# Per-head state reads of the sample sequences: summed with the in-sequence part in token rows, turned once, behind the chunk states

## The chip, the cores and the metric

The kernel runs on one core of one Trainium2 chip. The metric is the device time in microseconds of one execution. A NeuronCore has TensorE (PE: matrix products, whose results go to PSUM), VectorE (DVE), ScalarE (ACT), GpSimd (POOL) and SyncE (SP, here the issuer of most DMAs). Every engine works through its own list of instructions in order; semaphores are what lets one wait for another.

## What is computed

One inference step of two layers, for a prompt of 512 tokens and for eight sample sequences of 8 tokens each. The change lies in layer 0, a gated linear recurrence with 8 heads (key width 128, value width 256):

```python
# S_t = diag(f_t) S_{t-1} + k_t v_t^T,   o_t = S_t^T q_t      (per head, S is 128 x 256)
b = jnp.cumsum(gc, axis=2)
A = jnp.einsum('bhtc,bhsc,bhtsc->bhts', qc, kc, jnp.exp(rel))       # causal, within a chunk
o = (jnp.einsum('bhts,bhsv->bhtv', A, vc)                          # in-sequence part
     + jnp.einsum('bhtc,bhcv->bhtv', qc * jnp.exp(b), S))          # read of the state
S_new = exp(b_last) * S + jnp.einsum('bhsc,bhsv->bhcv', kc * jnp.exp(b_last - b), vc)
...
o = rmsnorm(o, g_norm_w);  y = (o * jax.nn.silu(z)) @ w_out
```

For the sample tokens S is the state that came in, one for each sequence and head. Layer 1 is a dilated sliding-window attention, which the change leaves alone.

## The kernel before

All tokens (512 + 64) lie along the free axis and features on the partitions; layer 0 goes head by head. The code of each engine is written out by hand, so the order on each engine is the order of the text. Step h (`pe_step`, `act_step`, `dve_step`) holds the input projections of head h, the scan of head g = h-1 and the norm of head f = h-2. Steps 1 to 7 have all three kinds of work but for edges; step 8 has the scan of head 7 without new projections.

On PE, step h projects (lines 367 and 388, weights split into a high and a low part, `PJ` being four PSUM banks that take projections in turns), with the products of the scan between them. The scan uses the other four banks, `X`. First come eight levels of masked products q·k (line 1043, "grams"), which DVE merges into `at` (prompt) and `ats` (the 64 sample tokens, 64x64). Then comes `pe_states`:

- line 1055, the state reads: for each of the eight sequences n, the queries `qz` (32 columns, of which 8 are the tokens of n and 24 are zeros) against the state `s0`. A product of 32 columns uses a quarter of TensorE's columns, and four of them, for n mod 4 = 0 to 3, lie side by side. The result has token rows: sequence n at partitions 32·(n mod 4), columns 256·(n // 4) of bank 0.
- lines 1060 and 1061: five transposes that turn the keys `kh` to token rows (bank 3, and bank 1 for the samples).
- lines 1067 and 1069: for each half of the 256 value features, the in-sequence part `v_`·`ats`, in feature rows, and onto it the reads, which ACT has copied out as `orow` (line 816) and a product with picked columns of the identity turns into feature rows. This makes six products, in bank 2 from column 384.
- line 1076: four products of keys and values, the chunk states (banks 0 and 1).

ACT copies `orow` (128x512), then `kr` (the turned keys, line 818), then `os_` (the sample outputs in feature rows, line 822), and goes on with the exponentials of the next head's levels 5 to 7 (line 775). DVE makes `kz` from the turned sample keys (line 943), and after two more levels the scan of chunk states (lines 973 and 975) from `up_ready`, then low parts of weights (line 340). PE goes on with projections; the sample states follow in two parts (line 1083), the first behind `os_done`. Every product of float32 operands stands in the trace as two records of matmul and weight load, a transpose as one.

Of the kernel before, what the change touches and what calls it, by code (L numbers as in the profile page):

```python
# [10 lines left out]
ALU = mybir.AluOpType  # L11
ACT = mybir.ActivationFunctionType
AX_X = mybir.AxisListType.X

P = 128
# [3 lines left out]
DB, DS = 8, 8  # L19
TS = DB * DS  # L20
# [8 lines left out]
AH, ADK, ADV = 8, 128, 256  # L29
QKW, VW = AH * ADK, AH * ADV  # L30
CH = TP // P
# [94 lines left out]
def program(nc, I, O):  # L126
    with ExitStack() as ctx:
        def sb(name, shape, dt=F32, stack=ctx):
            return stack.enter_context(nc.sbuf_tensor(name, shape, dt))

        def sem(name):
            return ctx.enter_context(nc.semaphore(name))
# [13 lines left out]
        ident = sb("ident", [P, P])  # L146
# [9 lines left out]
        X = ctx.enter_context(nc.psum_tensor("X", [P, 4, 512], F32))  # L156
# [12 lines left out]
        ones_done, c_sig, c_silu, c_t, c_sb = (sem(x) for x in "ones_done c_sig c_silu c_t c_sb".split())  # L169
# [5 lines left out]
        q_sig, z_sig, k_done, g_done, b_done, eb_done, dl_done, qe_done = (  # L175
            sem(x) for x in "q_sig z_sig k_done g_done b_done eb_done dl_done qe_done".split())
# [4 lines left out]
        up_ready, up_read, os_ready, os_done = sem("up_ready"), sem("up_read"), sem("os_ready"), sem("os_done")  # L181
        ua_ready, ua_read, ub_ready, ub_read = sem("ua_ready"), sem("ua_read"), sem("ub_ready"), sem("ub_read")
        orow_ready, orow_done = sem("orow_ready"), sem("orow_done")
        op_ready, sq_done, ms_ready, ms_read, r_done, fin_done = (
            sem(x) for x in "op_ready sq_done ms_ready ms_read r_done fin_done".split())
        s0_in, s0_out, sp_out = [sem("s0_in0"), sem("s0_in1")], [sem("s0_out0"), sem("s0_out1")], sem("sp_out")
# [56 lines left out]
        def ticket_w(h, t):  # L243
            return TICKETS * h + t
# [98 lines left out]
        def wait_read(eng, t):  # L343

            eng.wait_ge(pj_read[t % 2], t // 2 + 1)
# [341 lines left out]
        st = ExitStack()  # L687
# [13 lines left out]
        v_ = sb("v_", [P, 2, CH + 1, ADV], stack=st)  # L701
        s0 = sb("s0", [P, 2, DB, ADV], stack=st)
# [4 lines left out]
        ats = sb("ats", [TS, TS], stack=st)  # L707
# [4 lines left out]
        os_ = sb("os_", [P, 2, TS], stack=st)  # L712
        v_low = sb("v_low", [TS, ADV], stack=st)
        qz = sb("qz", [P, 2, DB, 32], stack=st)
        orow = sb("orow", [P, 2 * ADV], stack=st)
        adr = sb("adr", [P, 512], stack=st)
        st.close()
        cond.close()
# [15 lines left out]
        def pool_scan(pool, h):  # L734
            b = h % 2
            pool.wait_ge(dl_done, h + 1)
            wait_read(pool, ticket_w(h, 0))
            seqs = lambda ap: ap[:, TP:T].rearrange("p (n t) -> p n t", t=DS)
            nc.gpsimd.tensor_tensor(qz[:, b, :, 0:DS], seqs(qe[:, b]), seqs(q_[:, b]), ALU.mult).then_inc(qe_done, 1)
            nc.gpsimd.tensor_tensor(qe[:, b, 0:TP], qe[:, b, 0:TP], q_[:, b, 0:TP], ALU.mult).then_inc(qe_done, 1)  # L740
# [16 lines left out]
        def act_step(act, chain, h):  # L757
            b, g, f = h % 2, h - 1, h - 2
# [53 lines left out]
                act.activation(v_[:, b, 0:CH, :].rearrange("p c v -> p (c v)"),  # L812
                               PJ[:, 0:2, :].rearrange("p e n -> p (e n)"), ACT.Copy).then_inc(pj_read[0], 1)
            if scan:
                act.wait_ge(orow_ready, g + 1)
                act.activation(orow[:], X[:, 0, :], ACT.Copy).then_inc(orow_done, 1)
                act.wait_ge(kt_ready, g + 1)
                act.activation(kr[:].rearrange("p c k -> p (c k)"), X[:, 3, :], ACT.Copy).then_inc(kr_done, 1)
                act.wait_ge(os_ready, g + 1)
                if g >= 1:  # L820
                    act.wait_ge(fin_done, 2 * g)
                act.activation(os_[:], X[:, 2, 384:512].rearrange("p (j t) -> p j t", j=2), ACT.Copy).then_inc(os_done, 1)
# [224 lines left out]
        def pe_states(pe, g):  # L1047

            b = g % 2
            pe.wait_ge(gram_read, 8 * g + 8)  # L1050
            pe.wait_ge(s0_in[b], 16 * (g // 2 + 1))
            pe.wait_ge(qe_done, 2 * g + 2)
            for n in range(DB):
                q = n % 4 * 32
                last = pe.matmul(X[q:q + 32, 0, n // 4 * ADV:(n // 4 + 1) * ADV], qz[:, b, n], s0[:, b, n],
                                 start=True, stop=True)
            last.then_inc(orow_ready, 1)
            pe.wait_ge(lv_done, XS * g + XS)
            for c in range(CH):
                pe.transpose(X[:, 3, c * P:(c + 1) * P], kh[:, c * P:(c + 1) * P], ident[:])  # L1060
            pe.transpose(X[0:TS, 1, 0:P], kh[:, TP:T], ident[:]).then_inc(kt_ready, 1)
            wait_read(pe, ticket_w(g, 3))
            wait_read(pe, ticket_w(g, 2))
            pe.wait_ge(orow_done, g + 1)
            for j in range(2):
                c0 = 384 + j * TS
                pe.matmul(X[:, 2, c0:c0 + TS], v_[0:TS, b, CH, j * P:(j + 1) * P], ats[:], start=True, stop=False)
                for x in range(2):
                    last = pe.matmul(X[:, 2, c0 + 32 * x:c0 + 32 * x + 32],
                                     orow[:, x * ADV + j * P:x * ADV + (j + 1) * P],  # L1070
                                     ident[:].rearrange("p (i t) -> p i t", t=32)[:, :, 0:DS], start=False, stop=(x == 1))
            last.then_inc(os_ready, 1)
            pe.wait_ge(kr_done, g + 1)
            pe.wait_ge(kz_done, g + 1)
            for c in range(CH):
                last = pe.matmul(X[:, c // 2, c % 2 * ADV:(c % 2 + 1) * ADV], kr[:, c], v_[:, b, c], start=True, stop=True)  # L1076
            last.then_inc(up_ready, 1)

        def pe_new_states(pe, g, b0, bank, ready):
            for i in range(2):  # L1080
                for x in range(2):
                    r = slice(32 * x, 32 * x + 32)
                    last = pe.matmul(X[:, bank + x, i * ADV:(i + 1) * ADV], kz[r, b0 + i], v_[r, g % 2, CH],  # L1083
                                     start=True, stop=True)
            last.then_inc(ready, 1)
# [14 lines left out]
        def pe_step(pe, h):  # L1100
# [42 lines left out]
            if scan:  # L1143
                pe_states(pe, g)
# [451 lines left out]
        def own(buf, b):  # L1596

            c0 = 32 * b - DS * (b % 4)
            return buf.rearrange("p b t -> p (b t)")[:, c0:c0 + 32]
# [624 lines left out]
        def load_attention_constants(sp):  # L2224
            for dst, src in ((cs_raw[:, 0], I["c_cos"]), (cs_raw[:, 1], I["c_sin"]), (swaps, I["c_swap"]),
                             *((there, src) for _, there, src in masks),
                             (qkw[:, 0], I["b_q_norm_w"].partition_broadcast(P)),
                             (qkw[:, 1], I["b_k_norm_w"].partition_broadcast(P))):
                sp.dma_start(dst, src).then_inc(a_const, 16)
# [103 lines left out]
        @block.gpsimd  # L2333
        def _(pool):
            nc.gpsimd.memset(ones[:], 1.0).then_inc(ones_done, 1)
            nc.gpsimd.memset(eps[:], EPS).then_inc(ones_done, 1)
            nc.gpsimd.memset(scT[:], 0.0).then_inc(ones_done, 1)
            for n in range(3):
                s = n % 2 * 2
                pool.wait_ge(n_sq, 2 * n + 2)  # L2340
                nc.gpsimd.tensor_tensor(nsq[:, s], nsq[:, s], nsq[:, s + 1], ALU.add).then_inc(sq_sum, 1)
            pool.wait_ge(n_ms, 5)
            nc.gpsimd.memset(qz[:], 0.0).then_inc(ones_done, 1)
            pool.wait_ge(ones_done, 4)
            pool.wait_ge(parked, 16)
            for h in range(AH + 1):
                if h < AH:
                    pool_scan(pool, h)
                if 1 <= h <= AH - 2:
                    pool.wait_ge(sq_done, h)  # L2350
                    nc.gpsimd.tensor_tensor(sq0[:, 0], sq0[:, 0], sq0[:, 1], ALU.add).then_inc(sum_done, 1)
            pool.wait_ge(n_lo, 2 * KD + 1)
            pool.wait_ge(n_hx, 2 * KD + 1)
            pool.wait_ge(parked1, 16)
            nc.gpsimd.memset(qs, 0.0).then_inc(zeros_done, 1)
            nc.gpsimd.memset(pz[:], 0.0).then_inc(zeros_done, 1)
            pool.wait_ge(zeros_done, 1)
            pool.wait_ge(tab_done, 1)
            for j in range(GH):
                for g in range(3):  # L2360
                    for c in range(3):
                        rope_pool(pool, j, g, c)
                for g in range(3):
                    pool.wait_ge(qkt_read, 3 * j + g + 1)
                    if j or g:
                        pool.wait_ge(st_ready, 4 * j + (0, 1, 3)[g])
                    nc.gpsimd.tensor_copy(qs[:, :, 0:DS], qkT[:, g, 0, TP:T].rearrange("p (b t) -> p b t", b=DB)).then_inc(qs_done, 1)
# [130 lines left out]
```

## Time and profile before

| | us |
|---|---|
| median of three runs | 1216.82 (1215.17 to 1216.98) |
| the profiled execution, its own time | 1211.92 |
| its span, first to last instruction | 1210.1 |
| PE busy | 1166.0 (96%) |
| DVE / ACT / POOL busy | 644.1 (53%) / 508.9 (42%) / 147.2 (12%) |
| mean granted TensorE clock, share of full | 0.991 |

The profiled execution took 4.9 us less than the median of the timed ones. A busy engine is not one at its peak: TensorE's records overlap, so its pace is read from the distance between the starts of two groups.

### The profile page before, as it was taken

How to read it: one execution, taken by the hardware profiler on the slowest of the kernel's cores; microseconds unless marked ns; L12 is line 12 of the kernel's file. 1: busy time of each engine (PE TensorE's matmuls, PEld its weight loads, DVE VectorE, ACT ScalarE, POOL GpSimd, SP SyncE). 2: the span in 40 equal slices, each digit the busy share in tenths (PEclk: the TensorE clock that was granted, in tenths of full speed). 3: DMA queues.
4: the chain of work that ended last, by engine and by line, in shares of the span. 5: the costliest groups of instructions: out<-in, count | busy, mean ns of one | idle time of the engine just before them, and what ended most of it. 6: DMA issues, size and time to landing. Idle time of an engine off the chain costs nothing.

```text
span 1210.1 us, 23191 instructions
## 1 busy us (share of the span) xinstructions
PE 1166.0 (96%) x9624; PEld 1093.9 (90%) x9624; DVE 644.1 (53%) x1222; ACT 508.9 (42%) x1026; POOL 147.2 (12%) x155
## 2 busy tenths in 40 slices
PE   6889999999999999989999899999999999999998
PEld 4689998999998999988999799999999999998998
DVE  2775657575848474757333563364346335526432
ACT  3552344434443434353211364464356435537221
POOL 1000000000000000000000063045016204500000
PEclk9899999999999999999999899999999999999999
DMA  9862534343443434421622336423643282362432
GB/s 259 283 201 70 157 92 140 110 132 104 120 126 106 143 105 127 122 92 40 218 70 71 131 111 156 129 74 90 143 125 84 77 193 83 84 133 72 150 106 59
DMA packets 243067, 147.90 MB, mean 122 GB/s; under 512 B 19337, under 2 KB 237449, under 8 KB 242450
## 3 DMA queue, kind: packets, MB, share of 16 engines
q1 hardware_dynamic: 228626, 134.62, 39.6%
q10 hardware_dynamic: 14336, 11.80, 3.0%
q8 instruction: 76, 1.25, 0.4%
q14 instruction: 29, 0.24, 0.1%
HBM read 124.37 MB, written 22.02 MB: 121 GB/s over the span
## 4 chain that ended last, share of the span: by engine, by line
PE 89%; DVE 4%; DMA 3%; SPq 2%; ACT 2%; issue 1%; DVEq 0%; ACTq 0%
PE PJ L367 24%; PE PJ L1473 17%; PE PJ L1188 14%; PE PJ L388 8%; PE X L1043 5%; DMA raw<-in_a_w_in_dram 2%; PE PJ L414 1%; PE X L1166 1%; PE X L1589 1%; PE X L1083 1%; PE X L1076 1%; PE PJ L1498 1%; PE X L1554 1%; PE X L1616 1%; PE X L1168 1%; PE X L1097 1%
## 5 line engine op out<-in xcount | busy, mean ns | idle before, releaser
L340 DVE TENSOR_TENSOR w_lo<-raw,w_hi 128x1024 fp32r<-128x1024 f32 (+1 forms) x128 | 156.7, 1238 | 176.1 <-ACT w_hi L332 175.4
L332 ACT ACTIVATE w_hi<-raw 128x1024 fp32r<-128x1024 f32 (+1 forms) x128 | 129.1, 1025 | 157.5 <-PE PJ L1473 73.0
L1473 PE MATMUL PJ<-w_hi,h_hi 128*128 128x256 f32 x600 | 167.5, 287 | 0.8 <-DVE w_lo L340 0.7
L1473 PE MATMUL PJ<-w_lo,h_hi 128*128 128x256 f32 x600 | 164.5, 283 | 0.0
L367 PE MATMUL PJ<-h_hi,w_hi 128*128 128x288 f32 (+1 forms) x736 | 161.5, 301 | 0.9 <-ACT v_ L812 0.9
L367 PE MATMUL PJ<-h_hi,w_lo 128*128 128x288 f32 (+1 forms) x736 | 157.6, 296 | 0.0
L367 PE MATMUL PJ<-h_lo,w_hi 128*128 128x288 f32 (+1 forms) x736 | 157.3, 295 | 0.0
L1473 PE MATMUL PJ<-w_hi,h_lo 128*128 128x256 f32 x480 | 135.7, 283 | 0.0
L367 PEld LDWEIGHTS PJ<-h_hi,w_hi 128*128 128x128 f32 x736 | 118.0, 189 | 5.5 <-issue 4.5
L367 PEld LDWEIGHTS PJ<-h_hi,w_lo 128*128 128x128 f32 x736 | 118.9, 189 | 0.0
L367 PEld LDWEIGHTS PJ<-h_lo,w_hi 128*128 128x128 f32 x736 | 118.8, 189 | 0.0
L1473 PEld LDWEIGHTS PJ<-w_hi,h_hi 128*128 128x128 f32 x600 | 114.9, 192 | 2.1 <-DVE w_lo L340 0.9
L1473 PEld LDWEIGHTS PJ<-w_lo,h_hi 128*128 128x128 f32 x600 | 115.0, 192 | 0.0
L388 PE MATMUL PJ<-w_hi,h_hi 128*128 128x256 f32 x320 | 93.0, 298 | 4.2 <-DVE w_lo L340 4.2
L1188 PE MATMUL PJ<-oz_low,w_hi 128*128 128x256 f32 x448 | 96.1, 296 | 0.0
L1473 PEld LDWEIGHTS PJ<-w_hi,h_lo 128*128 128x128 f32 x480 | 92.0, 192 | 0.0
L388 PE MATMUL PJ<-w_lo,h_hi 128*128 128x256 f32 x320 | 88.5, 284 | 0.0
L1188 PEld LDWEIGHTS PJ<-oz_low,w_hi 128*128 128x128 f32 x448 | 75.6, 190 | 0.0
L388 PE MATMUL PJ<-w_hi,h_lo 128*128 128x256 f32 x256 | 72.9, 285 | 0.0
L1017 DVE SCALAR_TENSOR_TENSOR xT<-PJ,ada,xT 128x128 f32<-128x128 f32 (+1 forms) x40 | 17.7, 497 | 103.4 <-PE PJ L1188 96.7
L775 ACT ACTIVATE dd<-dd 128x576 f32<-128x576 f32 (+1 forms) x64 | 41.3, 657 | 72.3 <-DVE dd L878 63.2
L388 PEld LDWEIGHTS PJ<-w_hi,h_hi 128*128 128x128 f32 x320 | 61.9, 193 | 8.0 <-DVE w_lo L340 4.4
(309 smaller groups left out, 2286.5 us busy)
## 6 DMA issues: line engine op xcount, KB each, us to landing
raw<-in_a_w_in_dram SPq DMA_DIRECT2D x48, 512.0 KB, 4.3
raw<-in_ada_w_dram SPq DMA_DIRECT2D x32, 512.0 KB, 3.8
raw<-in_b_w_in_dram SPq DMA_DIRECT2D x64, 256.0 KB, 3.3
kvc<-in_cache_kv_w_dram SPq DMA_DIRECT2D x24, 512.0 KB, 5.3
pre<-in_ada_w_dram SPq DMA_DIRECT2D x16, 512.0 KB, 8.3
s<-in_state_hgrn_dram SPq DMA_DIRECT2D x8, 1024.0 KB, 7.0
out_hgrn_sample_dram<-s ACTq DMA_DIRECT2D x8, 1024.0 KB, 5.2
raw<-in_a_w_out_dram SPq DMA_DIRECT2D x16, 512.0 KB, 4.6
```

Of the source, the lines that this page charges most:

```text
L332: act.activation(w_hi[:, i % SPLITS, 0:size], raw[:, n % RAWS, 0:size], ACT.Copy).then_inc(hi_done, 1)
L340: dve.tensor_tensor(w_lo[:, i % SPLITS, 0:size], raw[:, n % RAWS, 0:size], w_hi[:, i % SPLITS, 0:size].bitcast(F32), ALU.subtract).then_in ...
L367: last = nc.tensor.matmul(PJ[:, 2 * s + e, 0:n1 - n0], a[:, k, :], b[:, k, n0:n1], start=(k == 0 and i == 0), stop=(k == KD - 1 and i == 2))
L388: last = nc.tensor.matmul(out_of(tile), a, b[:, k % 4, :], start=(k == 0 and i == 0), stop=(k == KD - 1 and i == len(passes) - 1))
L414: last = nc.tensor.matmul(PJ[q:q + 32, bank, n % 4 * P:n % 4 * P + P], scT[:, k, :], w[:, k, :], start=(k < 4), stop=(k >= 4))
L775: act.activation(dd[:, x % 2, 0:n], dd[:, x % 2, 0:n], ACT.Exp).then_inc(exp_done, 1)
L1017: dve.scalar_tensor_tensor(out=x, in0=y, scalar=gate, in1=x, op0=ALU.mult, op1=ALU.add)
L1043: last = pe.matmul(X[:, i % 2, c * P:(c + 1) * P], left[:, c * P:(c + 1) * P], right[:, c * P:(c + 1) * P], start=True, stop=True)
L1076: last = pe.matmul(X[:, c // 2, c % 2 * ADV:(c % 2 + 1) * ADV], kr[:, c], v_[:, b, c], start=True, stop=True)
L1083: last = pe.matmul(X[:, bank + x, i * ADV:(i + 1) * ADV], kz[r, b0 + i], v_[r, g % 2, CH], start=True, stop=True)
L1188: last = pe.matmul(PJ[:, 2 * (t % 2) + e, 0:z - x], a[:, n % nk, :], b[:, x:z], start=(n == 0 and i == 0), stop=(n == 2 * nk - 1 and i == 2))
L1473: last = pe.matmul(PJ[:, tile // 2, tile % 2 * 256:tile % 2 * 256 + 256], a, b[:, k, :], start=(first and k == 0 and i == 0), stop=(kk == ...
```

## The change

The reads no longer go to two column ranges of bank 0 but are added up, for the sequences of one quarter, in bank 2, columns 0 to 255. This needs each sequence's 8 query columns at another place of its 32; `own(qz, n)`, which layer 1 already used, takes a window that starts 8·(n mod 4) columns early and so brings them there. The rows of the 64 sample tokens are then 0 to 63, and the sequences are dealt over the four quarters so that two lie in each: quarters 0 and 1 hold four of the sequences, quarters 2 and 3 the other four in rows 64 to 127. The in-sequence part is now one product, `ats` by `v_`, in token rows 0 to 63 (line 1059 of the changed kernel), and the reads of quarters 0 and 1 are added onto it.

`orow` is now 128x256. A new constant `twice` (128x64, made once by POOL as the sum of the identity's two halves of columns) turns it: one product for each half of the value features both turns it and adds rows 64 to 127 onto rows 0 to 63. These two products stand behind the chunk states, the transposes ahead of the reads. ACT copies `kr` first, then `orow`.

```diff
         if scan:
-            act.wait_ge(orow_ready, g + 1)
-            act.activation(orow[:], X[:, 0, :], ACT.Copy).then_inc(orow_done, 1)
             act.wait_ge(kt_ready, g + 1)
             act.activation(kr[:].rearrange("p c k -> p (c k)"), X[:, 3, :], ACT.Copy).then_inc(kr_done, 1)
+            act.wait_ge(orow_ready, g + 1)
+            act.activation(orow[:], X[:, 2, 0:ADV], ACT.Copy).then_inc(orow_done, 1)
             act.wait_ge(os_ready, g + 1)
...
         pe.wait_ge(gram_read, 8 * g + 8)
-        pe.wait_ge(s0_in[b], 16 * (g // 2 + 1))
-        pe.wait_ge(qe_done, 2 * g + 2)
-        for n in range(DB):
-            q = n % 4 * 32
-            last = pe.matmul(X[q:q + 32, 0, n // 4 * ADV:(n // 4 + 1) * ADV], qz[:, b, n], s0[:, b, n],
-                             start=True, stop=True)
-        last.then_inc(orow_ready, 1)
         pe.wait_ge(lv_done, XS * g + XS)
...
         wait_read(pe, ticket_w(g, 3))
+        pe.wait_ge(s0_in[b], 16 * (g // 2 + 1))
+        pe.wait_ge(qe_done, 2 * g + 2)
+        pe.matmul(X[0:TS, 2, 0:ADV], ats[:], v_[0:TS, b, CH, :], start=True, stop=False)
+        for i in range(2):
+            for q in (2, 3, 0, 1):
+                n = q % 2 * 4 + q // 2 * 2 + i
+                last = pe.matmul(X[32 * q:32 * q + 32, 2, 0:ADV], own(qz[:, b], n), s0[:, b, n],
+                                 start=(i == 0 and q >= 2), stop=(i == 1))
+        last.then_inc(orow_ready, 1)
         wait_read(pe, ticket_w(g, 2))
-        pe.wait_ge(orow_done, g + 1)
-        for j in range(2):
-            c0 = 384 + j * TS
-            pe.matmul(X[:, 2, c0:c0 + TS], v_[0:TS, b, CH, j * P:(j + 1) * P], ats[:], start=True, stop=False)
-            for x in range(2):
-                last = pe.matmul(X[:, 2, c0 + 32 * x:c0 + 32 * x + 32],
-                                 orow[:, x * ADV + j * P:x * ADV + (j + 1) * P],
-                                 ident[:].rearrange("p (i t) -> p i t", t=32)[:, :, 0:DS], start=False, stop=(x == 1))
-        last.then_inc(os_ready, 1)
         pe.wait_ge(kr_done, g + 1)
         pe.wait_ge(kz_done, g + 1)
...
+        pe.wait_ge(orow_done, g + 1)
+        if g == 0:
+            pe.wait_ge(ones_done, 5)
+        for j in range(2):
+            last = pe.matmul(X[:, 2, 384 + j * TS:384 + (j + 1) * TS], orow[:, j * P:(j + 1) * P], twice[:],
+                             start=True, stop=True)
+        last.then_inc(os_ready, 1)
```

PE's list around `pe_states` of head 0, before. The names are the tiles written and read:

```order
L438 MATMUL PJ<-fold,adr 128x9 x3
L1055 MATMUL X<-s,qz 32x256 [waits qe_done,s0_in0,gram_read]
L1055 MATMUL X<-s,qz 32x256 x7
L1060 MATMUL X<-ident,kh 128x128 [waits lv_done]
L1060 MATMUL X<-ident,kh 128x128 x3
L1061 MATMUL X<-ident,kh 64x128
L1067 MATMUL X<-ats,v_ 128x64 [waits orow_done,pj_read0,pj_read1]
L1069 MATMUL X<-ident,orow 128x32 x2
L1067 MATMUL X<-ats,v_ 128x64
L1069 MATMUL X<-ident,orow 128x32 x2
L1076 MATMUL X<-v_,kr 128x256 [waits kz_done,kr_done]
L1076 MATMUL X<-v_,kr 128x256 x3
```

The same place in the changed kernel:

```order
L438 MATMUL PJ<-fold,adr 128x9 x3
L1054 MATMUL X<-ident,kh 128x128 [waits lv_done,gram_read]
L1054 MATMUL X<-ident,kh 128x128 x3
L1055 MATMUL X<-ident,kh 64x128
L1059 MATMUL X<-v_,ats 64x256 [waits qe_done,s0_in0,pj_read1]
L1063 MATMUL X<-s,qz 32x256 x8
L1070 MATMUL X<-v_,kr 128x256 [waits kz_done,kr_done,pj_read0]
L1070 MATMUL X<-v_,kr 128x256 x3
L1076 MATMUL X<-twice,orow 128x64 [waits ones_done,orow_done]
L1076 MATMUL X<-twice,orow 128x64
```

The transposes moved ahead of the reads, and the turning products, two instead of six, behind the chunk states. On ACT, before:

```order
L816 ACTIVATE orow<-X 128x512 [waits orow_ready]
L818 ACTIVATE kr<-X 128x512 [waits kt_ready]
L822 ACTIVATE os_<-X 128x128 [waits os_ready]
L775 ACTIVATE dd<-dd 128x512 [waits sub_done] x2
L775 ACTIVATE dd<-dd 128x576 [waits sub_done]
```

and in the changed kernel:

```order
L817 ACTIVATE kr<-X 128x512 [waits kt_ready]
L819 ACTIVATE orow<-X 128x256 [waits orow_ready]
L823 ACTIVATE os_<-X 128x128 [waits os_ready]
L776 ACTIVATE dd<-dd 128x512 [waits sub_done] x2
L776 ACTIVATE dd<-dd 128x576 [waits sub_done]
```

The two first copies changed places and one of them is half as wide; `os_` and the three exponentials behind it stand where they stood.

## Rows read from the trace of the kernel before

**Rows 1.** The page's first part: busy time and share of each engine.

```profile
PE 1166.0 (96%) x9624; PEld 1093.9 (90%) x9624; DVE 644.1 (53%) x1222; ACT 508.9 (42%) x1026; POOL 147.2 (12%) x155
```

**Rows 2.** Busy time in one head's period, from one L1055 to the next.

```profile
core 0: us, PE busy (x) PEld busy (x) DVE busy (x) ACT busy (x) POOL busy (x), PEclk, DMA share, GB/s
130.52:193.88 63.36, 63.12 (x538) 58.66 (x538) 40.14 (x78) 26.32 (x35) 3.34 (x3) 1.00 0.40 119
```

**Rows 3.** Timeline of PE, head 1: start us, length us, line, tiles, form, records.

```profile
192.89 1.06 PE L438 MATMUL PJ<-fold,adr 128*128 128x9 f32 x8
193.88 1.07 PE L1055 MATMUL X<-s,qz 128*32 128x256 f32 x16
194.88 0.66 PE L1060 MATMUL X<-ident,kh 128*128 128x128 f32 x4
195.37 0.27 PE L1061 MATMUL X<-ident,kh 128*64 128x128 f32 x1
195.76 0.40 PE L1067 MATMUL X<-ats,v_ 64*128 64x64 f32 x2
196.09 0.63 PE L1069 MATMUL X<-ident,orow 128*128 128x32 f32 x4
196.66 0.43 PE L1067 MATMUL X<-ats,v_ 64*128 64x64 f32 x2
197.02 0.63 PE L1069 MATMUL X<-ident,orow 128*128 128x32 f32 x4
197.48 1.97 PE L1076 MATMUL X<-v_,kr 128*128 128x256 f32 x8
199.11 0.47 PE L388 MATMUL PJ<-w_hi,h_hi 128*128 128x256 f32 x1
199.41 0.28 PE L388 MATMUL PJ<-w_lo,h_hi 128*128 128x256 f32 x1
199.53 0.28 PE L388 MATMUL PJ<-w_hi,h_hi 128*128 128x256 f32 x1
```

**Rows 4.** Timeline of PE in layer 1, columns as in rows 3.

```profile
854.67 0.43 PE L1694 MATMUL X<-vr,oz 64*64 64x128 f32 x2
855.03 1.08 PE L1700 MATMUL X<-kvc,pz 128*32 128x128 f32 x32
856.04 1.09 PE L1589 MATMUL X<-ident,kvc 128*128 128x128 f32 x8
856.97 1.00 PE L1708 MATMUL X<-ident,oz 128*128 128x64 f32 x8
857.79 0.50 PE L367 MATMUL PJ<-h_hi,w_hi 128*128 128x256 f32 x2
```

**Rows 5.** Timeline of ACT in the same head; in brackets, idle us before and releaser.

```profile
195.02 0.60 ACT L816 ACTIVATE orow<-X 128x512 f32<-128x512 f32 x1 [1.57 <-PE X L1055]
195.68 0.60 ACT L818 ACTIVATE kr<-X 128x512 f32<-128x512 f32 x1
197.69 0.28 ACT L822 ACTIVATE os_<-X 128x128 f32<-128x128 f32 x1 [1.41 <-PE X L1069]
...
208.56 0.65 ACT L769 ACTIVATE oz<-PJ 128x576 f32<-128x576 f32 x1 [2.76 <-PE PJ L367]
```

**Rows 6.** Timeline of DVE in the same head.

```profile
195.68 0.68 DVE L943 TENSOR_TENSOR kz<-X,seqm 64x512 f32<-64x512 f32 x1 [1.50 <-PE X L1061]
...
203.61 2.35 DVE L340 TENSOR_TENSOR w_lo<-raw,w_hi 128x1024 fp32r<-128x1024 f32 x2
209.24 0.76 DVE L898 TENSOR_TENSOR oz<-PJ,oz 128x576 f32<-128x576 f32 x1 [3.29 <-ACT oz L769]
```

**Rows 7.** What SP's DMA queue waited for, 100 to 560 us: total, times, longest.

```profile
SPq L2292 <- PE PJ L414: 180.0, 28, 9.4
```

**Rows 8.** Timeline of ACT, then PE, in the last head.

```profile
557.68 0.28 ACT L822 ACTIVATE os_<-X 128x128 f32<-128x128 f32 x1 [1.41 <-PE X L1069]
...
559.38 1.13 PE L1083 MATMUL X<-v_,kz 32*128 32x256 f32 x8
```

More of the change, by code:

```diff
@@ L714, in program @@
         qz = sb("qz", [P, 2, DB, 32], stack=st)
-        orow = sb("orow", [P, 2 * ADV], stack=st)
+        orow = sb("orow", [P, ADV], stack=st)
+        twice = sb("twice", [P, TS], stack=st)
         adr = sb("adr", [P, 512], stack=st)
@@ L2345, in _ @@
             pool.wait_ge(parked, 16)
+            nc.gpsimd.tensor_tensor(twice[:], ident[:, 0:TS], ident[:, TS:P], ALU.add).then_inc(ones_done, 1)
             for h in range(AH + 1):
```

## The prediction, made before the changed kernel was run

> **What bounds the kernel now.** I read the shares first: PE is busy 96% of the span, DVE 53%, ACT 42% [rows 1]. A share is an average, so the next view is the busy time of one head's period. From one state read (L1055) to the next there are 63.36 us, the same to 0.01 us in six periods, of which one is shown, and PE is busy for 63.12 of them at the full granted clock; ACT works 26 us, DVE 40 us, the DMA engines are busy 0.40 of the time [rows 2]. So in layer 0 PE waits for nobody once it is under way, and what leaves its list leaves the time, unless something else becomes late. The third view is the timeline of PE through `pe_states` of one head [rows 3]; the same groups stand in all eight heads. The fourth is a place in layer 1 with the very kinds of products that the change brings [rows 4].
>
> The lengths in a timeline overlap, so I price by distances between starts. From the first read (193.88) to the second projection product behind the chunk states (199.41) there are 5.53 us. I take the second because the first L388 record is shown as starting before the chunk states are through: 0.30 us lie between the two where the next follows at 0.12.
>
> **What a change of shape costs.** The four records of L1069 stand twice in rows 3: from 196.09 to 196.66 (0.57 us) with a product of another form behind them (64 rows of the array instead of 128), and from 197.02 to 197.48 (0.46) with one of the same form. Leaving a form costs 0.11 us. Entering one costs something too, since its first weights can't be loaded under the work ahead: the four L1060 records take 0.49, at 0.11 each 0.44, so 0.05. L438 (8 records, 0.99) and L1708 (8 records, 0.82) differ by 0.17, about half at each end [rows 3, 4].
> The Trainium skill has a rule on this: the page TensorEngine Tiling, Key Properties, says that switching the tiling mode, other than going to another tile of the same mode, drains TensorE. The two L1069 groups agree with it for 128 to 64 rows. By that rule alone, counting forms in the two orders, seven switches become four, which speaks for the change, with about a third of the sum below; L1061 (64 columns behind 128) counts as a switch by it and shows none of the cost, in both kernels.
>
> **The changed stretch, term by term, per head.**
> - Entry. The transposes follow L438 in the same form, where the reads changed it. That saves 0.08 ahead of 193.88 (half of the 0.17), and the first load is hidden: the four transposes take 0.44.
> - The fifth transpose and the change to 64x64: 0.11 + 0.11, less a little as only 64 weight columns are loaded; 0.20. Before, 0.39 passed here (195.37 to 195.76), since PE waited for `orow`, whose copy ends at 195.62 [rows 5]. That wait is gone.
> - `ats` by `v_` in token rows, two records of 256 columns. No such row exists. L1694 is the same form with 128 columns and also has the 32-column reads behind it: 0.36 for two [rows 4]. 16 records of 256 columns (L1055) take 1.00 and 32 of 128 columns (L1700) take 1.01, both four abreast, so a step of 256 columns costs as much as two of 128, which is 0.11 more per record: 0.58. Bounds: 0.36, were it hidden beside the reads of the other two quarters, and 0.80.
> - The eight reads, 16 records: 1.00, as now with another form behind. That they add up in one bank makes no difference in L1700, which adds four such products in each quarter and runs at the pace named.
> - The chunk states. Now 197.48 to 199.41 less one step of 0.12: 1.81. They will follow a change of form, so 0.02 to 0.10 more; their first step is already a long one, I take 1.83. Their waits: the turned keys are ready about 0.8 us after the first transpose (194.88 to 195.68, where DVE starts on them) [rows 3, 6], and `kr` and `kz` take 0.60 and 0.68. Counted from the first transpose that is 1.4 and 1.5, while PE gets to the chunk states at 0.44+0.20+0.58+1.00 = 2.22. Covered, with 0.7 to spare; if `ats` and the reads took only 0.9 together, PE would begin to wait here.
> - The turning: two products of 64 columns, four records, at the pace of L1708 (0.82 for 8, nearly all of it one load each): 0.45. Its wait: `orow` can be copied once the reads have ended, with half the columns some 0.4 us (between the 0.28 of `os_` and the 0.60 of 512 columns), which lies beside the 1.83 of the chunk states. Covered.
> - The projection behind: from its first to its second product 0.20, an estimate between the 0.12 of its pace and the 0.30 of now [rows 3].
>
> The sum is 0.44+0.20+0.58+1.00+1.83+0.45+0.20 = 4.70, against 5.53, with 0.08 at the entry: **0.91 us less per head**. With the bounds of the terms it is 0.6 to 1.15.
>
> **Heads 0 to 6** sit inside steps with projections: 7 x 0.91 = 6.4 us.
>
> **The last head** has no projection behind; PE goes straight to L1083, which waits for `os_done`. Before, `os_` was copied by 557.96 under the chunk states [rows 8]. Now the turning is the last thing ahead of the wait, and behind its last record come its end (0.28), the copy (0.28) and two hand-overs, 0.7 us, where 0.33 were spent from the last chunk state. DVE also has oz_low to make ahead of `kz` there, which may keep PE 0.1 us. I put the gain at 0.2, bounds -0.2 and 0.5.
>
> **What the move makes late.** `os_ready` comes behind the chunk states. Before, ACT started `os_` at 197.69 [rows 5]; by the terms above the turning ends near 198.5, so ACT starts it 0.85 later, and three exponentials that are queued behind it, DVE's levels on these, its scan of the chunk states and its two low halves of weights (L340, 203.61 to 205.96) move by up to as much. DVE waits behind them 3.29 us for PE's projection by way of ACT, and ACT waits 2.76 itself [rows 5, 6]. PE now comes 0.91 earlier, so that these two waits shrink by about 1.8 and stay positive. The projection that needs the first low half starts behind that same wait, so it finds it there with over 1 us to spare. I cost the delay at nothing; the cover is 1.0 to 1.5 us. `kz` and `kr` are earlier by about 1.0, which helps DVE. The loads: SP's queue waits for PE to free buffers (180.0 us in 28 waits) [rows 7], so weights are not what is late. The new POOL instruction is 64 columns, once, where POOL has nothing else; it stands ahead of the `qz` of head 0, for which PE waits before anyway.
>
> **Sum.** 6.4 + 0.2 = 6.6 us. The profiled execution would go from 1211.92 to 1205.3 (its span from 1210.1 to 1203.5). The median shown is 4.9 us above the profiled one, nothing in the profile says why, and I take the same difference from it: 1216.82 - 6.6 = 1210.2, 0.54% less.
>
> **Rivals.**
> - Slower: the reads lose their four-abreast running, because the two rounds now write the same columns of a bank and two quarters add onto what `ats` left. Then 16 records go one after another at the pace of L1076 (1.81 for 8, 0.22 each): 3.6 instead of 1.00, 2.6 more, and 0.91 becomes a loss of 1.7 per head; times 8, 13.5 us: 1230. It turns the sign from the point where `ats` and reads take over 2.5 us together. L1700 does exactly this adding without such a loss [rows 4], with one difference: there each 64x64 product stands in the same chain as well. 4 in 100.
> - No change: ACT's late `os_`. If the 0.85 reached PE in each of the seven heads (through the exponentials, DVE and the low half of weights), 7 x 0.06 + 0.2 = 0.6 would be left: 1216.2. It needs the cover of 1.0 to 1.5 us worked out above to be false, for instance because ACT's other pieces don't move up with PE. 7 in 100.
> - Half the gain: something small waits in each head (chunk states for `kr` or `kz`, the turning for `orow`, or each change of form costs 0.1 more around the new order). 0.3 to 0.6 per head, 2.4 to 4.8 us: near 1213. 12 in 100.
> - The forecast: 0.6 to 1.15 per head, 4.5 to 8.5 us, 1208.3 to 1212.3: 77 in 100.
>
> **How the numbers follow.** The three timed runs before lie within 1.8 us, so the median of after can be off by about 1 us whatever the kernel; that widens the low end to 1207.6. The high end takes in part of the half-gain case: 1213.4. What a measurement can tell from no change is 0.2%, 2.4 us. Faster by over that: the forecast and most of the half-gain case, 0.86. Within: the late `os_` and the rest of it, 0.10. Slower: 0.04.
>
> **What would show it.** In the profile of the changed kernel: a head's period of 62.4 to 62.5 us instead of 63.36, with PE busy all but 0.2 of it; the reads at 1.0 us and not 3.6; about 0.58 from the `ats` product to the reads; the turning at 0.45; ACT's wait at its L769 row down from 2.76 to about 1, DVE's at the gate down by 1.8, and no new wait of PE. The forecast is wrong if PE shows idle time ahead of a projection, with DVE's low halves as the releaser, or if the step from one form to the next is longer than 0.2 us anywhere in the stretch.

## The result, and the profile after

The changed kernel takes 1207.16 us (median of 8 runs, 1204.88 to 1211.51) against 1214.88 us for the kernel before (8 runs on the same chips, 1212.12 to 1216.98): a ratio of 0.9938, 95% interval 0.9923 to 0.9952. It is faster by about 0.6%; the two medians lie 7.7 us apart. The prediction said faster, by 0.54% and 6.6 us, but gave the time as 1210.2 with a range of 1207.6 to 1213.4, and 1207.16 lies below that. What it said of the mechanism held in the main; its range for the time did not.

One head's period (busy time between two first transposes; start and end, length, then busy time and records of each engine, granted clock, DMA share) in the changed kernel:

```profile
core 0: us, PE busy (x) PEld busy (x) DVE busy (x) ACT busy (x) POOL busy (x), PEclk, DMA share, GB/s
130.98:193.37 62.39, 62.26 (x533) 57.66 (x533) 40.13 (x78) 26.11 (x35) 3.34 (x3) 1.00 0.39 116
```

This answers to [rows 2]: 62.39 for 63.36, the same in all six full periods, and PE still busy for all but 0.13 us. The saving is 0.97 us per head.

PE's timeline through the changed stretch of head 1, which answers to [rows 3]:

```profile
192.46 1.06 PE L438 MATMUL PJ<-fold,adr 128*128 128x9 f32 x8
193.37 0.63 PE L1054 MATMUL X<-ident,kh 128*128 128x128 f32 x4
193.84 0.27 PE L1055 MATMUL X<-ident,kh 128*64 128x128 f32 x1
194.04 0.64 PE L1059 MATMUL X<-v_,ats 64*64 64x256 f32 x2
194.62 1.07 PE L1063 MATMUL X<-s,qz 128*32 128x256 f32 x16
195.62 1.99 PE L1070 MATMUL X<-v_,kr 128*128 128x256 f32 x8
197.45 0.56 PE L1076 MATMUL X<-twice,orow 128*128 128x64 f32 x4
197.81 0.37 PE L388 MATMUL PJ<-w_hi,h_hi 128*128 128x256 f32 x1
198.02 0.28 PE L388 MATMUL PJ<-w_lo,h_hi 128*128 128x256 f32 x1
```

From start to start, against the terms of the sum:

| term | predicted | before | after |
|---|---|---|---|
| L438 to the next group | 0.08 less | 0.99 | 0.91 |
| four transposes | 0.44 | 0.49 | 0.47 |
| fifth transpose and what follows | 0.20 | 0.39 | 0.20 |
| `ats` by `v_` in token rows | 0.58 | - | 0.58 |
| reads | 1.00 | 1.00 | 1.00 |
| six turning products | - | 1.72 | - |
| chunk states | 1.83 | 1.63 | 1.83 |
| two turning products | 0.45 | - | 0.36 |
| first to second L388 | 0.20 | 0.30 | 0.21 |

ACT and DVE in the same head, which answer to [rows 5] and [rows 6] (in brackets the idle time before and what ended it):

```profile
194.15 0.60 ACT L817 ACTIVATE kr<-X 128x512 f32<-128x512 f32 x1 [1.14 <-PE X L1055]
195.76 0.38 ACT L819 ACTIVATE orow<-X 128x256 f32<-128x256 f32 x1 [1.01 <-PE X L1063]
198.04 0.28 ACT L823 ACTIVATE os_<-X 128x128 f32<-128x128 f32 x1 [1.90 <-PE X L1076]
...
207.16 0.65 ACT L770 ACTIVATE oz<-PJ 128x576 f32<-128x576 f32 x1 [1.73 <-PE PJ L367]
```

```profile
198.87 0.43 DVE L751 TENSOR_TENSOR qk<-k_,dd 128x256 f32<-128x256 f32 x1 [3.37 <-ACT dd L776]
...
207.84 0.76 DVE L899 TENSOR_TENSOR oz<-PJ,oz 128x576 f32<-128x576 f32 x1 [1.53 <-ACT oz L770]
```

In the kernel before, DVE's wait for the exponentials was 1.48:

```profile
198.51 0.43 DVE L750 TENSOR_TENSOR qk<-k_,dd 128x256 f32<-128x256 f32 x1 [1.48 <-ACT dd L775]
```

The copy of `orow` ends at 196.14, 1.3 us before PE needs it. `os_` starts 0.35 later by the time since the start of the span, and counted from L438, 0.78 later than before (5.58 for 4.80); DVE now waits 3.37 us for the exponentials. The waits for the projection further on took it up: DVE's (1.53, where it was 3.29) and ACT's (1.73, where it was 2.76). ACT's shrank by only 1.0 and not by the 1.8 that were forecast, because two shorter waits of ACT on its way there, of 0.55 and 0.22 us in the kernel before, are gone as well.

The last head, PE:

```profile
550.67 0.66 PE L1054 MATMUL X<-ident,kh 128*128 128x128 f32 x4
...
554.77 0.55 PE L1076 MATMUL X<-twice,orow 128*128 128x64 f32 x4
555.69 1.13 PE L1084 MATMUL X<-v_,kz 32*128 32x256 f32 x8 [0.37 <-ACT os_ L823]
```

From the start of the stretch to the sample states there are 5.02 us, where there were 5.51 (553.87 in the trace of before to 559.38 [rows 8]): 0.49 less, with the new wait for `os_` of 0.37 in it. Seven heads and the last give 7 x 0.97 + 0.49 = 7.3 us.

The span of this profiled execution is only 3.6 us shorter (1206.5 for 1210.1). The granted clock tells why. Ten-microsecond windows of the step with the last head, changed kernel, columns as above:

```profile
520.00:530.00 10.00, 8.83 (x61) 8.38 (x58) 4.10 (x10) 2.74 (x4) 0.00 (x0) 0.83 0.37 126
530.00:540.00 10.00, 7.52 (x51) 6.37 (x50) 7.63 (x11) 8.87 (x13) 0.00 (x0) 1.00 0.19 54
540.00:550.00 10.00, 8.47 (x61) 7.84 (x61) 5.56 (x12) 3.09 (x6) 0.00 (x0) 0.83 0.00 0
```

and in the trace of the kernel before:

```profile
520.00:530.00 10.00, 8.83 (x70) 8.12 (x69) 5.47 (x12) 2.26 (x3) 0.00 (x0) 1.00 0.39 115
530.00:540.00 10.00, 10.00 (x71) 9.04 (x71) 3.58 (x5) 7.36 (x9) 0.00 (x0) 1.00 0.49 159
540.00:550.00 10.00, 6.08 (x53) 5.57 (x52) 8.11 (x15) 7.33 (x13) 0.00 (x0) 1.00 0.00 0
```

The mean granted clock stands third from the end of a line, as a share of the full 2.4 GHz. A mean of 0.83 means that for a third of such a window the clock was at its lower level, 1.2 GHz. Shortly ahead of the first of these stretches PE had waited 1.2 us for DVE, and the second began in the last 0.3 us of a wait of 2.8 us; both waits stand in both kernels. From the starts of the same groups in both traces, the first cost 1.6 us and the second 1.4. The first scan products came 0.5 later (108.12 for 107.59); there too the clock was lower, a mean of 0.89 between 60 and 90 us for 0.94. -7.3 + 1.6 + 1.4 + 0.5, with the decimals kept, is the -3.7 us at which the two traces stand when layer 0's output projection begins, and they keep it to the end.

### The profile page after: what moved, and what is told of

It is laid out like the page before. It is cut to its first block, busy times and chain, and to the rows that moved or that the text cites. A ratio compares the mean times of both kernels' runs of the same rounds, so it can differ in the third digit from the quotient of the medians.

```text
span 1206.5 us, 23097 instructions
## 1 busy us (share of the span) xinstructions
PE 1162.4 (96%) x9576; PEld 1089.3 (90%) x9576; DVE 644.3 (53%) x1222; ACT 507.6 (42%) x1026; POOL 147.5 (12%) x156
## 4 chain that ended last, share of the span: by engine, by line
PE 89%; DVE 3%; SPq 3%; DMA 2%; ACT 1%; issue 1%; DVEq 0%; ACTq 0%
PE PJ L367 24%; PE PJ L1474 17%; PE PJ L1189 14%; PE PJ L388 8%; PE X L1044 5%; PE X L1167 1%; PE PJ L414 1%; PE X L1590 1%; PE X L1070 1%; PE X L1084 1%; PE PJ L1499 1%; PE X L1555 1%; PE X L1617 1%; PE X L1169 1%; DMA raw<-in_a_w_in_dram 1%; PE X L1098 1%
## 5 line engine op out<-in xcount | busy, mean ns | idle before, releaser
L388 PE MATMUL PJ<-w_hi,h_hi 128*128 128x256 f32 x320 | 92.8, 298 | 4.3 <-DVE w_lo L340 4.3
L388 PE MATMUL PJ<-w_lo,h_hi 128*128 128x256 f32 x320 | 89.0, 286 | 0.0
L388 PE MATMUL PJ<-w_hi,h_lo 128*128 128x256 f32 x256 | 73.5, 287 | 0.0
L388 PEld LDWEIGHTS PJ<-w_hi,h_hi 128*128 128x128 f32 x320 | 62.4, 195 | 7.9 <-DVE w_lo L340 4.5
```

The costliest lines, as they stand in the source:

```text
L388: last = nc.tensor.matmul(out_of(tile), a, b[:, k % 4, :], start=(k == 0 and i == 0), stop=(k == KD - 1 and i == len(passes) - 1))
```

## The experiments

Every kernel's period is that of its own profile. Where the clock stays at its upper level it repeats to 0.01 or 0.02 us in all heads but the first, so one execution is enough to read it. Where no number of runs is given, the kernel was executed once.

**The changed kernel again.**

> The changed kernel once more, with timed rounds. In its first profile a head's period is 62.39 us against 63.36, so seven heads and the last one should give 7 x 0.97 + 0.5 = 7.3 us, but its span is only 3.6 us shorter, because the granted clock fell twice near step 8 and the start came 0.6 us later. Theory one (the dips of the clock belong to a single execution and not to the kernel): the period is 62.39 again, the step 8 that follows runs without the two dips or with dips at another place, and over the timed runs the time goes with the mean granted clock, 0.984 near 1210 and 0.991 near 1204; ratio 0.994. Theory two (the changed kernel has brought the dips, by lower activity in its step 8): both dips are there again at the same places and cost 2.5 us, and the ratio stays near 0.997.

Measured: 1206.11 us (6 runs, 1203.77 to 1207.68) against 1215.10 (17 runs, 1212.02 to 1217.89), ratio 0.9930 (0.9915 to 0.9944). The period is 62.39 again and the terms are the same to 0.001. One low stretch stands in the same place of step 8, the second moved to 580 us:

```profile
520.00:530.00 10.00, 8.83 (x61) 8.38 (x58) 4.10 (x10) 2.77 (x4) 0.00 (x0) 0.83 0.37 125
...
540.00:550.00 10.00, 8.39 (x70) 7.62 (x70) 6.93 (x14) 3.06 (x6) 0.00 (x0) 1.00 0.00 1
580.00:590.00 10.00, 8.09 (x50) 7.86 (x49) 3.58 (x7) 2.58 (x3) 0.00 (x0) 0.83 0.91 249
```

Theory one holds for the second stretch; for the first, at the same place twice, the two traces alone don't decide. The eight timed runs of the changed kernel in the result show that time goes with the mean granted clock: spans of 1204.0 and 1204.3 at 0.991, 1203.2 at 0.990, 1203.0 at 0.989, 1206.5 and 1207.0 at 0.987, 1208.8 at 0.986, 1209.7 at 0.984, or about 0.8 us for each 0.001. Over all timed runs the clock favours neither kernel: its mean is 0.9885 in the 14 runs of the changed kernel and 0.9884 in the 17 of the kernel before, while their mean spans differ by 7.8 us (1205.1 and 1213.0). So the low stretches scatter the times but don't make the difference.

**The kernel before, again.**

> The kernel before once more, for the granted clock. In its first trace the clock has no low stretch between 60 and 670 us from the start of PE's work; the changed kernel has one at 516.8 and one at 533.9, its repeat one at 516.3 and one at 577.7. Theory (low stretches fall where PE is idle for some of the time, as it is from step 8 on, and whether one falls there is a matter of the single execution): a low stretch may stand between 510 and 600 us here too, and heads have a period of 63.36 whatever it does. Rival (the kernel before is free of them, and the change brings one): none between 60 and 670 us again.

Measured: 1216.14 us, 4.2 more than its first profiled execution, all periods 63.36 (or 0.01 less).

```profile
60.00:90.00 30.00, 24.34 (x214) 23.01 (x215) 21.87 (x45) 17.21 (x22) 2.14 (x2) 0.89 0.69 199
...
520.00:560.00 40.00, 34.72 (x276) 31.20 (x274) 24.21 (x43) 19.63 (x28) 0.00 (x0) 0.96 0.23 70
```

In the first trace the same windows had 0.94 and 1.00. The first scan products came 3.1 us later, of which the low stretch that is new there explains a part, and the low stretch in step 8 cost 1.5. So the kernel before has them too, and the rival (the change brings them) falls. The trace of `four_turns` below, a kernel close to the changed one, has none in step 8. Why its first profiled execution was 4.9 us under the median of its three timed runs is shown by this in part: it was spared both stretches.

**The order alone.** The old computation, in the new order (ACT's copies too are in the order of the changed kernel):

```diff
             pe.wait_ge(gram_read, 8 * g + 8)
-            (eight reads into bank 0)
+            (transposes, as they were; then the eight reads, into bank 2)
...
+            for c in range(CH):
+                last = pe.matmul(X[:, c // 2, ...], kr[:, c], v_[:, b, c], start=True, stop=True)
+            last.then_inc(up_ready, 1)
             pe.wait_ge(orow_done, g + 1)
-            (six turning products into bank 2, then the chunk states)
+            (six turning products into bank 3)
```

> The kernel before with the changed order alone: transposes ahead of the reads, chunk states, then the old six turning products behind them; reads in bank 2, the turned output in bank 3. Theory (the gain is the sum of an order part and a form part): order part per head = 0.08 at the entry, 0.05 of a load no longer seen, 0.19 of PE's wait for orow; the number of changes of form stays as it was, since the order ends on 128-row products as before, so 0.3 us per head, period 63.05 and 2.2 us in all. Rival (the order is what brings it, since the wait for orow is larger than the trace shows): period near 62.6. Second rival (the late os_ copy costs as much as the order gains): period 63.36.

Measured: period 63.29, 0.07 less than before and not 0.3. The timed runs gave 1217.75 us, ratio 1.0025 (1.0011 to 1.0038). PE in head 1:

```profile
195.00 1.07 PE L1059 MATMUL X<-s,qz 128*32 128x256 f32 x16
196.01 1.99 PE L1067 MATMUL X<-v_,kr 128*128 128x256 f32 x8
197.93 0.43 PE L1072 MATMUL X<-ats,v_ 64*128 64x64 f32 x2
198.29 0.63 PE L1074 MATMUL X<-ident,orow 128*128 128x32 f32 x4
```

The expected parts came (0.08 at the entry, 0.02 of a load, 0.19 of the wait), but my expectation counted changes of form and not which groups stand beside them. The chunk states, which had one neighbour of their own form on either side, now have another form on both: 1.92 to the next group, where the prediction had read 1.81 for the kernel before, and the projection behind starts on a product that shows its first load. That gave back 0.2. So the order alone brings 0.07 of the 0.97 us per head; the other 0.90 need the smaller turning and its form, which also lets the chunk states keep a neighbour of their own form. That the whole kernel is slower by 0.25% comes in part from its last head, where PE waits 0.5 us for `kz` and 0.4 for `os_`, while its seven heads save 0.5: about 0.4 us more. The mean granted clock of its ten timed runs is 0.9866, for 0.9884 in the 17 of the kernel before; at 0.8 us for each 0.001 that is an estimated 1.4 us. Together they make 1.8, inside the interval of 1.3 to 4.6 us that was measured. Whether the lower clock belongs to this order or to these ten runs is not shown.

**The turning in front of the chunk states again.**

```diff
+            (wait for orow_done; the two turning products)
             pe.wait_ge(kr_done, g + 1)
             pe.wait_ge(kz_done, g + 1)
...
-            (wait for orow_done; the two turning products)
```

> The changed kernel with the two turning products put back ahead of the chunk states. Theory: PE then waits for the copy of orow, which ends 0.38 + 0.1 us after the reads' last result; chunk states began 1.00 after the first read, the turning could begin at 1.55 to 1.6, so the period grows by 0.55 to 0.6, to 62.95. Rival (placement is worth nothing, since the chunk states too wait for something): period 62.39 still. Rival on ACT: os_ and the exponentials come 1.3 us earlier, so if their lateness cost anything the period would be below 62.9.

Measured: period 63.02 or 63.03 (62.98 in the first head), 0.63 more.

```profile
195.36 1.07 PE L1063 MATMUL X<-s,qz 128*32 128x256 f32 x16
197.03 0.63 PE L1071 MATMUL X<-twice,orow 128*128 128x64 f32 x4 [0.59 <-ACT orow L819]
```

PE waits 0.59 us for the copy of `orow`. So the place of the two products is worth 0.63 to the new computation, while the order was worth only 0.07 to the old one: there the transposes stood between the reads and the turning and hid all but 0.19 of the copy. In this kernel, with the new computation, the transposes already ahead of the reads and the turning still ahead of the chunk states, 0.34 of the 0.97 us are there; neither the computation nor the order makes the gain by itself.

**Four turning products for two.**

```diff
             for j in range(2):
-                last = pe.matmul(X[:, 2, 384 + j * TS:...], orow[:, j * P:(j + 1) * P], twice[:],
-                                 start=True, stop=True)
+                for x in range(2):
+                    last = pe.matmul(X[:, 2, 384 + j * TS:...], orow[:, j * P:(j + 1) * P],
+                                     ident[:, x * TS:(x + 1) * TS], start=(x == 0), stop=(x == 1))
```

> The changed kernel without the constant that adds the two halves: each half of the value features is turned by two products that add up, with columns 0 to 63 and 64 to 127 of the identity, so four products (8 records) instead of two (4). Theory (the turning is paced by its weight loads, 0.11 each): 0.44 to 0.46 more per head, period 62.84. Rival (weights of the same tile needn't be seen twice, or the records start under the chunk states): below 0.3 more, period under 62.7.

Measured: period 62.84 (0.45 more), as the theory had it.

```profile
198.26 1.00 PE L1077 MATMUL X<-ident,orow 128*128 128x64 f32 x8
199.07 0.37 PE L388 MATMUL PJ<-w_hi,h_hi 128*128 128x256 f32 x1
```

The eight records take 0.81 where four take 0.36, so each further one costs 0.11. The constant `twice` is worth 0.45 of the 0.97.

**Reads in pairs of one quarter.**

```diff
-            for i in range(2):
-                for q in (2, 3, 0, 1):
+            for q in (2, 3, 0, 1):
+                for i in range(2):
```

> The changed kernel with the eight reads in another order: the two of one quarter directly behind each other (quarters 2, 2, 3, 3, 0, 0, 1, 1) instead of round the four quarters. Theory (the order round the quarters is what keeps four abreast, products start in the list's order): a product and the next one on the same quarter can't overlap, so at best one quarter's second runs beside the next one's first, and 16 records take at least 9 steps of 0.216 instead of 4: 1.9 to 2.1 us and not 1.00, period 62.39 + 0.95 to 1.1 = 63.4. Rival (TensorE hands products to idle quarters whatever their order): 1.00 and 62.39. Rival (all overlap is lost): 3.5 us and period 64.9, the price that the prediction gave the case slower than before.

Measured: period 62.41, 0.02 more. PE:

```profile
195.42 1.09 PE L1063 MATMUL X<-s,qz 128*32 128x256 f32 x16
196.44 1.99 PE L1070 MATMUL X<-v_,kr 128*128 128x256 f32 x8
```

1.02 us instead of 1.00. The first rival holds: with two products of one quarter directly behind each other in the list, the 16 records still start in four groups of four, 0.22 us from group to group. The prediction's case of a slower kernel rested on another danger, that reads which add up in one place lose this; the changed kernel itself, with its reads at 1.00, shows that they don't.

**The in-sequence product in the form of the reads**, a candidate beyond the change. `put` makes one product into a quarter of bank 2, `seq` gives the sequence that stands there:

```diff
-            pe.matmul(X[0:TS, 2, 0:ADV], ats[:], v_[0:TS, b, CH, :], start=True, stop=False)
-            (reads, i = 0 and 1, in quarters 2, 3, 0, 1)
+            for q in range(2):
+                put(q, ats[:, 32 * q:32 * q + 32], v_[:, b, CH, :], True, False)
+            for q, i in ((2, 0), (3, 0), (0, 0), (1, 0), (2, 1), (3, 1), (0, 1), (1, 1)):
+                n = seq(q, i)
+                last = put(q, own(qz[:, b], n), s0[:, b, n], i == 0 and q >= 2, i == 1)
...
+            nc.gpsimd.memset(ats[TS:P], 0.0).then_inc(ones_done, 1)
+            (and v_[TS:P, b, CH, :], for both buffers)
```

> A candidate beyond the change: the in-sequence product is given the form of the reads (ats padded to 128 rows with zeros, in two products of 32 columns for quarters 0 and 1), so that all ten products have one form. Theory (a change of form costs 0.1 and the 64x64 product stands alone on the array for its whole time): from the fifth transpose to the chunk states 10 products in 4 quarters make three rounds of two steps of 0.216, so 1.43 with the exit instead of 0.58 + 1.00 = 1.58, and the entry keeps its cost: period 62.39 - 0.15 = 62.24; the best case, a fourth round fully hidden, is 62.1. Rival (products of one quarter that follow each other in a chain stall the array): period at or above 62.39.

Measured: period 62.23 to 62.24, and 1204.69 us (6 runs, 1203.28 to 1207.40), ratio to the kernel before 0.9922 (0.9906 to 0.9938).

```profile
193.67 0.41 PE L1061 MATMUL X<-v_,ats 128*32 128x256 f32 x2
193.68 0.41 PE L1061 MATMUL X<-s,qz 128*32 128x256 f32 x2
193.91 0.39 PE L1061 MATMUL X<-v_,ats 128*32 128x256 f32 x2
193.92 1.24 PE L1061 MATMUL X<-s,qz 128*32 128x256 f32 x14
195.09 1.99 PE L1074 MATMUL X<-v_,kr 128*128 128x256 f32 x8
```

From 193.67 to 195.09 there are 1.42 us for all ten products, against 0.58 + 1.00, as worked out. In the first lines `ats` and the reads of the other quarters run side by side, which they did not in two forms. The profile shows 0.15 us per head less than the changed kernel; the timed medians (1204.69 and 1206.11; the intervals of their ratios to the kernel before overlap) agree in sign but can't settle 1.2 us.

**How late ACT may be.** Idle copies of 512 columns ahead of the exponentials that stand behind `os_`:

```diff
             if new and scan:
+                for n in range(8):
+                    chain(act.activation(idle[:], kr[:].rearrange("p c k -> p (c k)"), ACT.Copy))
                 level_exps(5, XS)
```

> The changed kernel with eight idle copies of 512 columns on ACT between os_ and the exponentials behind it, in the steps that have new projections; each waits for the one before, so 0.6 to 0.7 each and 5.0 to 5.5 us in all. It puts a price on the cover of the late os_. In the first trace of the changed kernel DVE's first low half of weights is ready at 205.2 and PE needs it at 208.1, so the cover is 2.9 us. Theory: 5.2 - 2.9 = 2.3 us of it reach PE per head, period 64.7, and PE's wait names DVE's low halves (L340). Rival (cover 1.0 to 1.5, as the prediction had it): period 66.2. Rival (ACT's lateness does not reach PE at all, since loads and low halves are far ahead): period 62.39.

Measured: periods of 65.0 to 67.5 us. Who waited for whom between 130 and 520 us (total, times, longest):

```profile
DVE qk L752 <- ACT dd L777: 52.1, 6, 8.7
...
PE PJ L367 <- DVE w_lo L340: 15.4, 6, 2.6
```

DVE's wait grew from 3.37 to 8.7, so the copies took 5.3; PE waited 2.6 of it per head, so 2.7 are covered, and the low half of weights is the place, as named. But the period grew by 4.1 us in most heads and not by 2.6. Two windows of 66 us in this trace have a granted clock of 0.95 and 0.97, and the last full period one of 1.00:

```profile
195.00:261.00 66.00, 63.31 (x522) 58.77 (x520) 38.49 (x76) 30.52 (x42) 3.34 (x3) 0.95 0.38 114
261.00:327.00 66.00, 63.31 (x531) 58.76 (x527) 39.68 (x78) 31.16 (x43) 3.34 (x3) 0.97 0.38 114
464.92:529.90 64.98, 62.29 (x533) 57.63 (x533) 39.98 (x78) 31.16 (x43) 3.34 (x3) 1.00 0.39 117
```

Inside the heads of the changed kernel it is 1.00. The last period, 64.98, is 2.6 longer than 62.39: the wait and nothing else, which settles the cover. Each of the five periods ahead of it holds a stretch at 1.2 GHz that begins during the wait of 2.6 us or within 1.5 us of its end, and is longer than 64.98 by 1.3 to 1.6 us, or by 2.5 (67.5) where the low stretch is the longest.

With four copies:

> As the eight idle copies on ACT, with four, which took 2.6 to 2.7 us in the run with eight (DVE's longest wait for the exponentials grew from 3.4 to 8.7 us, so 5.3 for eight). With eight, PE waited 2.6 us per head for DVE's low half of weights, so 2.7 of the 5.3 were covered. Theory: 2.65 us are covered whole or all but 0.1, period 62.4 to 62.5, no low stretch of the clock inside the heads. Rival (cover 1.0 to 1.5 as the prediction had it; the eight copies showed less since something else gave way): PE waits 1.2 per head, period 63.6.

Measured: period 62.39, and DVE waits up to 6.0:

```profile
DVE qk L752 <- ACT dd L777: 42.1, 7, 6.0
```

2.65 us of delay cost nothing at all. So of the cover that `os_`'s new place draws on, about 2.7 us are left unused.

## Why the prediction was right, and where it was wrong

**What bounds the kernel** was right: PE's list is the time, and 0.97 us less of it per head is 0.97 us less period.

**The terms.** Seven of the eight that the table prices were right to 0.03 us. The form of the `ats` product (0.58) and the chunk states behind a change of form (1.83), for which the trace of before had no row, came out on the value taken from the nearest rows. The turning products were over-priced: 0.45 for 0.36. The step that failed was to price all four records at 0.11. In the trace the second starts only 0.06 behind the first, and the projection 0.08 behind the last. The row that it was read from says the same: the eight records of L1708 take 0.82 and not eight times 0.11, and four fewer at 0.11 make 0.37. In all 0.97 for 0.91.

**The last head** gained 0.49 for 0.2, at the top of its bounds. The wait for `os_` was there with 0.37, which is what the prediction's 0.7 for 0.33 comes to, and DVE's oz_low did not hold up `kz`. The 0.2 did not follow from its own terms: 0.91 less 0.37, and less the 0.1 set aside for `kz`, leaves over 0.4, and no term is given for the rest.

**The late `os_`** was covered, as forecast. The size was off: the cover was put at 1.0 to 1.5 us, and 2.7 are left. In the trace of the changed kernel the first low half is ready at 205.2, and PE starts the projection that needs it at 208.1. ACT's wait did not go down to about 1, as said above.

**The slower case** (reads losing their four-abreast running) did not come, with 1.00 for the reads; in pairs they take 1.02.

**The rule on tiling modes** from the Trainium skill (TensorEngine Tiling, Key Properties) was borne out in sign by the `ats` product: in its own form it takes 0.58 alone, and in the form of the reads it runs beside them. The fifth transpose does not bear it out, in the changed kernel as in the one before: its 64 columns start 0.11 behind the last transpose of 128, at the pace of the others.

**The range** is where the prediction failed. The mechanism gave 7.3 us, 0.7 more than forecast. Of the rest of the 3.0 us between 1210.2 and 1207.16, 1.9 are the level of the kernel before, and 0.4 are within the scatter of the medians. The step that failed, "the three timed runs before lie within 1.8 us, so the median of after can be off by about 1 us", took the spread of three runs for that of the kernel. In 8 runs its median is 1214.88, 1.9 less than the three gave, and 17 runs reach from 1212.02 to 1217.89. The profiled execution, 4.9 us below the three, had already shown that a single kernel moves by more than 1.8. I passed over it with "nothing in the profile says why"; the granted clock was the place to look, and half of that difference, given to the level, would have widened the low end to about 1205. Against the 1214.88 the forecast saving gives 1208.3, 1.1 above what was measured.

## What to carry to other kernels

Where TensorE's list is the time, a change to it can be priced to within 0.1 us, here term by term and in its sum, from starts of groups in the same trace, if each group is taken with its neighbours: here a product of another form beside it cost 0.02 to 0.1 us where the form was entered and about 0.1 where it was left, and giving neighbours one form, with zeros in the operand, saved 0.15 us per head by the profile. A row that gives the price of a group is taken with its ends: eight records of 0.82 are not twice four. A copy that PE waits for is best placed under long products that don't need it: here the place was worth 0.63. And before a range is put around a time, look whether the granted clock differs between executions of the kernel as it is: here spans of the changed kernel reach from 1203.0 to 1209.7 with it, more than most of these edits move them.

## What the hardware showed that was not expected

- Products of 32 columns ran four abreast in both orders that were tried: 1.02 us for pairs of one quarter, 1.00 for a round of the quarters.
- A wait of 2.6 us inside an otherwise full PE came with a low stretch of the clock in five of the six full periods of the kernel with eight idle copies, at 1.3 to 2.5 us beside the 2.6 of the wait.
- In the stretch from 510 to 640 us, where PE waits 1.2, 2.8 and about 2 us in every kernel (3.2 for the first of them with eight idle copies), the eleven traces have 13 low stretches, none in two of them and one or two in each other. Twelve of the 13 begin within 1.5 us of the start of the first product behind a wait of 1.2 us or more; the one at 561 us of the kernel with the order alone does not. Most such waits are without one, with the same length in the same place. What decides it was not tried.
